# Where xhi and xlo lie in SBUF, in a two-layer encoder trunk on one core

## The reference

```
x += 0.5 * swiglu(rmsnorm(x), ffn1)           # gate and up 1024 x 2816, down 2816 x 1024
h  = rmsnorm(x) @ w_in                        # 2320 columns: q, k, v, GLA q, k, v, gate, r
x += concat(sliding_window_attention(h), gated_linear_attention(h)) @ w_out
x += 0.5 * swiglu(rmsnorm(x), ffn2)
```

## Time and profile before

| | before |
|---|---|
| time, median of 3 runs | 1013.82 us (1010.22 to 1018.42) |
| span of the profiled execution | 1017.0 us |
| mean granted TensorE clock | 0.975 |
| PE busy, PEld busy | 982.7 us, 968.6 us |
| DVE, ACT, POOL busy | 628.1, 457.6, 57.7 us |
| DMA | 169.13 MB, 166 GB/s |

### The profile page before, as it was taken

How to read it: one execution, slowest core, us unless ns; L and a number is a source line. 1 busy time by engine, 2 the same in 40 slices (tenths; PEclk the granted TensorE clock), 3 DMA queues, 4 the chain that set the end, 5 groups by cost and what they waited for, 6 DMA issues and landing times.

```text
span 1017.0 us, 20058 instructions
## 1 busy us (share of the span) xinstructions
PE 982.7 (97%) x8116; PEld 968.6 (95%) x8116; DVE 628.1 (62%) x743; ACT 457.6 (45%) x499; POOL 57.7 (6%) x37
## 2 busy tenths in 40 slices
PE   6999999989999999999979999998999999999996
PEld 6999999989899999999979999998998999999996
DVE  7756565667768655555666555557495685555553
ACT  5443434536635434343543434345385444343432
POOL 3000000030101000000110000003001030000000
PEclk9999999999979999999989999999998999999997
DMA  7665656544326655555536555555531446556531
GB/s 246 227 193 178 194 177 198 167 135 125 84 64 214 195 191 182 190 180 191 166 133 208 175 196 173 198 175 155 169 87 63 157 156 212 197 174 197 172 117 43
DMA packets 130620, 169.13 MB, mean 166 GB/s; under 512 B 3216, under 2 KB 116112, under 8 KB 130576
## 3 DMA queue, kind: packets, MB, share of 16 engines
q1 hardware_dynamic: 130576, 168.52, 52.3%
HBM read 167.46 MB, written 1.05 MB: 166 GB/s over the span
## 4 chain that ended last, share of the span: by engine, by line
PE 61%; issue 31%; DVE 4%; POOL 3%; DMA 1%; ACT 0%; SPq 0%; POOLq 0%; DVEq 0%; ACTq 0%
PE ps L358 19%; PE ps L360 19%; PE ps L359 19%; POOL sq L1346 2%; DVE xlo L982 2%; PE ps L668 1%; PE ps L664 1%; DVE wlo L977 1%; DMA raw<-in_ffn_w_gate 1%; POOL sqsum_a L1346 0%; DVE resid L1004 0%; PE ps L415 0%; PE ps L738 0%; PE ps L706 0%; DVE wlo L993 0%
## 5 line engine op out<-in xcount | busy, mean ns | idle before, releaser
L358 PE MATMUL ps<-xhi,whi 128*128 128x256 f32 x1760 | 505.0, 287 | 14.1 <-DVE wlo L993 7.2
L977 DVE TENSOR_TENSOR wlo<-raw,whi 128x2048 fp32r<-128x2048 f32 (+1 forms) x159 | 357.1, 2249 | 253.8 <-ACT whi L756 253.8
L360 PE MATMUL ps<-xhi,wlo 128*128 128x256 f32 x1760 | 500.8, 285 | 0.0
L359 PE MATMUL ps<-xlo,whi 128*128 128x256 f32 x1760 | 500.7, 284 | 0.0
L756 ACT ACTIVATE whi<-raw 128x2048 fp32r<-128x2048 f32 (+1 forms) x159 | 297.2, 1869 | 188.5 <-PE ps L360 181.7
L358 PEld LDWEIGHTS ps<-xhi,whi 128*128 128x128 f32 x1760 | 340.3, 193 | 18.2 <-DVE wlo L993 6.6
L359 PEld LDWEIGHTS ps<-xlo,whi 128*128 128x128 f32 x1760 | 340.6, 194 | 0.1
L360 PEld LDWEIGHTS ps<-xhi,wlo 128*128 128x128 f32 x1760 | 340.2, 193 | 0.0
L358 PE MATMUL ps<-h_parts,whi 128*128 128x256 f32 x704 | 194.7, 277 | 0.0
L359 PE MATMUL ps<-h_parts,whi 128*128 128x256 f32 x704 | 194.6, 276 | 0.0
L360 PE MATMUL ps<-h_parts,wlo 128*128 128x256 f32 x704 | 194.4, 276 | 0.0
(11 more groups left out here) (138 smaller groups left out, 530.0 us busy)
## 6 DMA issues: line engine op xcount, KB each, us to landing
raw<-in_ffn_w_down SPq DMA_DIRECT2D x44, 1024.0 KB, 4.9
raw<-in_ffn_w_up SPq DMA_DIRECT2D x43, 1024.0 KB, 5.3
raw<-in_ffn_w_gate SPq DMA_DIRECT2D x42, 1024.0 KB, 5.4
raw<-in_w_in SPq DMA_DIRECT2D x12, 1024.0 KB, 5.2
raw<-in_w_in SPq DMA_DIRECT2D x8, 512.0 KB, 4.5
raw<-in_w_out SPq DMA_DIRECT2D x8, 512.0 KB, 4.1
raw<-in_w_in SPq DMA_DIRECT2D x2, 1088.0 KB, 5.2
raw<-in_ffn_w_gate SPq DMA_DIRECT2D x8, 256.0 KB, 7.6
```

What stands on the lines that cost most here:

```text
L358: pe.matmul(o, w_hi, x_hi, start=start, stop=False, skip_group_check=True)
L359: pe.matmul(o, w_hi, x_lo, start=False, stop=False, skip_group_check=True)
L360: return pe.matmul(o, w_lo, x_hi, start=False, stop=stop, skip_group_check=True)
L977: nc.vector.tensor_tensor(lo, r, h.bitcast(F32), ALU.subtract).then_inc(lo_done, 1)
```

## The change

Two pairs of tiles of 16384 bytes in all trade places: xhi and xlo (8192 bytes each) with S (12288) and qT (4096). No instruction, size, wait or order is changed.

```
-        xhi = sb("xhi", [P, KT, SEQ], F32R)
-        xlo = sb("xlo", [P, KT, SEQ], F32R)
+        S = sb("S", [P, HEADS, 3 * P])
+        qT = sb("qT", [P, 4, SEQ])
         sq = sb("sq", [P, KT, SEQ])
...
         kv = sb("kv", [P, 2, SEQ])
-        qT = sb("qT", [P, 4, SEQ])
+        xhi = sb("xhi", [P, KT, SEQ], F32R)
+        xlo = sb("xlo", [P, KT, SEQ], F32R)
...
-        S = sb("S", [P, HEADS, 3 * P])
         PT = sb("PT", [P, HEADS, 3 * P])
```

## The result

The changed kernel took **1006.41 us** (996.17 to 1013.68, 17 runs), the kernel before 1013.82 (1007.09 to 1018.42, 17 runs beside them). The ratio is 0.9909 (95% interval 0.9887 to 0.9931): 7 us in place of the 28 predicted, outside the range of 979 to 1000. The profiled execution of the changed kernel has a span of 1001.5 us against 1017.0: these two lie 15.5 us apart, twice as far as the medians, so what differs between them is not all the change.

A forecast was written before the change was run, and what follows sets the result against it. TensorE was taken to set the end, at its cost per matmul. Terms 21.6 + 2.85 + 3.5 = 27.9, about 28 us, off the median 1013.8 gave 986 us, range 979 to 1000.

The forecast's parts named there:

- xhi and xlo behind 131072: Feed-forward loops: x matmuls fall from 119.8 to h's 113.5 ns, 0.60 us a body, 36 bodies, 21.6 us.
- the 2.85 us ahead of the loops: 120 x matmuls after the sums, before each feed-forward loop: 0.75 us each, less 24 at half clock, 2.85 us gained.
- the prediction's own signs: In the loop: x and h at the same distance of starts, near 113.4 ns, body 16.3 to 16.4 us; w_out at 113.4.
- the forecast's worst case: Low end of the forecast's own gain: 23 us if the mixers give nothing back, 991 us, with the spread 995.
- No change: Whole kernel: place does not matter, h's 6.3 ns come from something else; gain 0, time 1013.8 us; chance 0.08.
- The loop gets another bound: Feed-forward loop: DMA loads could end last, body about 16.7 us or half the gain lost; 1000 us; chance 0.10.
- Slower: Feed-forward x units: writes of h hold up reads of x, 58.2 us added, 28 gained; 1044 us; chance 0.05.
- Where it is lost: Mixer starts, KG and R0 (0.6 us), half of R1, some w_out, between parts: faster TensorE only waits longer for other engines.
- What was put down for the mixers: Q0, Q1, QG 0.90 us, half of R1 0.15, part of w_out 0.68: 1.73 us, 3.5 for both layers.
- S and qT: VectorE and ScalarE operations on these tiles, moved before 131072: put at 0, bounds -0.5 and +0.5 us.
- Token-major units: V1 units with x stationary and weights moving: 0.2 us a layer if the pair counts, else nothing; put at 0.

The follow-up runs named there:

- all behind: The changed kernel with whi, wlo, xhi, xlo and h_parts all placed behind byte 131072: 1025.27 us.
- the second trace of the changed kernel: The changed kernel executed once more with no further edit, to get another trace: 999.07 us.

## Why the prediction was wrong

**The step that failed** is the first term of "xhi and xlo behind 131072": 0.60 us a loop body, 21.6 us in all. The price was taken from 96 matmuls of h, 113.5 ns, as if a pair on different sides had one price. It has two, 113.3 and 117.8, and the loop went to the second. Measured: x 11.30 us a body where 10.90 was forecast, and h 5.66 where it had been 5.46, together nothing. The same price stands in the 2.85 us ahead of the loops: the 72 of x between spread and loop in part 1 took 8.48 us in place of 8.64, 0.16 less where 0.45 was counted. Of the prediction's own signs, x and h at the same distance came, near 113.4 ns did not. With one long matmul behind each spread the same loop gives 0.64 us a body, 23.0 us in all: the term was there to be had, and the sum of 28 was of the right size for that kernel (33 us against the runs beside it).

**What showed it beforehand, and was misread.** The earlier trace rows were used as a witness for the sides. What the spread does to the matmuls behind it was not asked, though in the kernel before x stands at 120 on both sides of it and could show nothing. Nor could the 0.24 us of its two matmuls: with starts given to 0.01 us that is 115 to 125 ns each, which holds 117.8 as well as 120. No row of the trace before has 117.8 as a steady pace. So the range should have held the case that h's pace does not carry over. (By its own terms, 21.6 + 2.85, the forecast's worst case is 24.45 us and not 23; nothing hangs on it.)

**The mechanism** was right in its core: place sets the price, and the pair counts, not the moving operand's side alone (17.28 us a body with h near the weights, 17.28 with all behind). The direction was right.

**No change**, the rival by the rule of the Trainium skill ("TensorE: Matmul & The Clock Gate", "Part 2: What happens when you issue a matmul"): two independent SBUF read ports, so that loading the next weights takes no read bandwidth from the running matmul. The page says nothing of place; taken, as in the prediction, to mean that place does not matter, the rule does not hold here: h moved alone went from 113.8 to 120.0 ns. That the two reads meet in SBUF would fit the runs, but no run separates a meeting of reads from another cause tied to place.

**The loop gets another bound** did not happen as put: at a body of 16.32 us the DMAs and the splits kept up. The loop did get another pace, on TensorE itself, which no rival had.

**Slower**, by writes of h holding up reads of x, is refuted by the same body: h is written there on the side from which x is read, and the pace is 113.3 throughout.

**"Where it is lost"** was half right for the softmax of mixer 0. From the first scores (242.01 in the earlier trace rows, 236.93 after) TensorE reaches the transposes 20.00 us later in place of 20.63, so the 0.6 us of KG and R0 came; the products behind the transposes (L604) then took 0.93 us where they took 0.65, and the linear attention's sums (L641) began 28.46 us after the first scores in place of 28.81. Some 0.3 of the 0.6 were given back, not all. What was put down for the mixers, 3.5 us, is less than the 5.9 by which the distances of x fell there at full clock; the waits took part of that back.

**"S and qT"**: the 0 was right, but not by the fit: two unknowns always fit two rows. The operations on the moved tiles show it: VectorE writes S (L1139) in 481 ns where it took 482, and qT (L1125) in 681 where it took 680. **"Token-major units"**: one of mixer 0 went from 5.93 to 5.85 us, within the 0.2 us allowed; its steady distance fell from 120 to 117.8 ns, with x as the stationary operand.

## What to carry to other kernels

Put stationary and moving operands of fp32r streams of 256 columns on different sides of SBUF, and then read the distance of starts in the loop itself, in the new kernel: a pace measured in one unit does not carry over to another. Where a loop is slower than the same tiles are elsewhere in the same trace, look at the last odd matmul ahead of it, its place and its width; one more matmul a part was worth 28 us here. Where a kernel has two paces, compare executions part by part before its median is explained.

## What the hardware showed that was not expected

- Three steady paces of one instruction at granted clock 1.0: 113.3 ns, 117.8 (one weight load in three at 192 ns), 120 (all at 192). The middle one is kept for a whole part, 163 us, across x and h, until something disturbs it.
- A stretch at granted clock 0.5 can end with a quicker pace than it found. In the second trace of the changed kernel, the matmuls just ahead of the one at part 3 (517.28 to 518.22) stand 117.5 ns apart on average and those behind it 113.3. All four traces with such a stretch at the head of part 3 came out of it at 113.3 (the others ran at 113.3 up to a wait in front of it); elsewhere streams came out at 117.8, as at 22.4 us in the changed kernel.
- With x apart from the weights, one 512-column matmul in an unbroken stream left the other of the two paces, ten times of ten; a pair of 256 columns left 117.8 whatever it found with ones_r at 133696, and what it found with ones_r at 94848. Why, and why either pace holds itself up, no run here tells.
